# Twelve conditioning slots in one place, and sums that stay in PSUM to the end: a two-block transformer forward on one core

## The reference, cut to what matters

```python
for l in range(2):                                   # block 1
    h = rms_norm(x, norm_mix_pre[l])
    ...                                              # 12 slices of h @ w_in[l]: conformer conv, stick-breaking
    mix = concat([y_conf, y_sb, y_ret, y_sc]) @ w_out[l]   # attention, retention, short conv
    x = x + rms_norm(mix, norm_mix_post[l])
    f = conv_ffn(rms_norm(x, norm_ffn_pre[l]), ffn_up[l], ffn_conv_w[l], ffn_down[l])
    x = x + rms_norm(f, norm_ffn_post[l])
# block 2: c and c_ctx condition it through ada = silu(c) @ ada_w + ada_b, six vectors of 1024
shift1, scale1, g1, shift2, scale2, g2 = split(ada, 6)
u, uc = modulate(rmsnorm(x, norm1_g), shift1, scale1), modulate(rmsnorm(ctx, norm1_g), ...)
x = x + g1 * token_mixer(u, uc, ...)                 # mLSTM both ways, differential attention, branches, w_o
u2 = modulate(rmsnorm(x, norm2_g), shift2, scale2)
x = x + g2 * moe_ffn(u2, ...)                        # 32 experts, the 4 best per token, gated, with biases b2
out = rmsnorm(x, final_g)
```

## Time and profile before

| | |
|---|---|
| median of 3 runs | 2231.74 us (2228.82 to 2232.68) |
| the profiled execution | 2231.71 us, span 2229.9 us |
| mean granted TensorE clock | 0.974 of full speed |
| PE busy | 2046.9 us, 92% of the span |
| DVE, ACT busy | 849.1 us (38%), 610.5 us (27%) |
| DMA | 589.67 MB, mean 264 GB/s |
| GB/s by fortieth of the span | 48 to 328 in the 17th to the 24th, 416 in the 25th, 431 to 433 from the 26th to the 39th |

### The profile page before, as it was taken

The page is one execution under the profiler, slowest core; times in us unless marked ns, Lnnn a source line. Parts: engine busy times, 40 slices in busy tenths (PEclk is TensorE's granted clock), DMA queues, the critical chain, the costliest instruction groups (busy, mean ns, idle before and its releaser), DMA issues.

```text
span 2229.9 us, 27760 instructions
## 1 busy us (share of the span) xinstructions
PE 2046.9 (92%) x11052; PEld 1322.1 (59%) x11052; DVE 849.1 (38%) x1484; ACT 610.5 (27%) x976; POOL 11.6 (1%) x23
## 2 busy tenths in 40 slices
PE   8879999986999799899989999999999999999997
PEld 7838997963999677677779633333333333333332
DVE  5546676663677624744542221111111111111112
ACT  4425555532555523143441110000000000000001
POOL 0000000001000000000000000000000000000000
PEclk9989999998999999899999999999999999999999
DMA  7435553436654325012223679999999999999996
GB/s 286 189 151 181 191 189 134 163 132 219 229 189 164 120 76 198 0 48 95 76 95 151 254 328 416 431 432 431 431 433 431 431 431 432 432 432 432 432 432 258
DMA packets 42081, 589.67 MB, mean 264 GB/s; under 512 B 5120, under 2 KB 5936, under 8 KB 8544
## 3 DMA queue, kind: packets, MB, share of 16 engines
q1 hardware_dynamic: 40304, 583.17, 64.1%
q0 software_dynamic: 1392, 4.93, 0.8%
q10 hardware_dynamic: 288, 0.24, 0.1%
HBM read 587.28 MB, written 1.05 MB: 264 GB/s over the span
## 4 chain that ended last, share of the span: by engine, by line
PE 76%; DMA 12%; DVE 6%; issue 3%; ACT 2%; DVEq 0%; SPq 0%; ACTq 0%
PE psum L1856 45%; PE psum L2247 21%; DMA slots<-exp_w_dram 11%; PE psum L2227 3%; PE psum L2378 3%; PE psum L2284 3%; DVE work L1812 1%; DMA slots<-ffn_up_dram 1%; DVE split_weights L1440 1%; DVE work L1557 0%; DVE split_weights L1260 0%; PE psum L1876 0%; ACT work L889 0%; PE psum L2132 0%; DVE work L1574 0%
## 5 line engine op out<-in xcount | busy, mean ns | idle before, releaser
L2247 PE MATMUL psum<-slots,work 128*64 128x512 f32 x3072 | 676.4, 594 | 60.1 <-DVE work L1812 24.8
L1856 PE MATMUL psum<-split_rows,split_weights 128*128 128x256 f32 (+1 forms) x3744 | 497.4, 295 | 22.9 <-DVE split_weights L1260 11.1
L1856 PEld LDWEIGHTS psum<-split_rows,split_weights 128*128 128x128 f32 x3744 | 478.9, 195 | 46.2 <-DVE split_weights L1260 13.7
L2247 PEld LDWEIGHTS psum<-slots,work 128*64 128x64 f32 x3072 | 219.5, 137 | 481.7 <-issue 480.5
L1260 DVE TENSOR_TENSOR split_weights<-slots,split_weights 128x1024 fp32r<-128x1024 f32 x180 | 218.9, 1223 | 184.0 <-ACT split_weights L922 183.8
L922 ACT ACTIVATE split_weights<-slots 128x1024 fp32r<-128x1024 f32 x180 | 189.6, 1058 | 258.4 <-PE psum L1856 185.6
L1856 PE MATMUL psum<-split_weights,split_rows 128*128 128x512 f32 x1008 | 234.0, 392 | 0.0
L1856 PEld LDWEIGHTS psum<-split_weights,split_rows 128*128 128x128 f32 x1008 | 189.7, 189 | 40.3 <-issue 0.8
L903 ACT ACTIVATE work<-psum 128x512 f32<-128x512 f32 (+3 forms) x182 | 95.6, 536 | 396.2 <-PE psum L2247 254.4
L1817 DVE TENSOR_SCALAR work<-psum 128x512 f32<-128x512 f32 x32 | 22.0, 688 | 424.5 <-PE psum L2247 424.5
L1171 ACT ACTIVATE work<-work 128x512 f32<-128x512 f32 x32 | 20.2, 631 | 499.4 <-DVE work L1817 499.4
(11 more groups left out here) (248 smaller groups left out, 1293.4 us busy)
## 6 DMA issues: line engine op xcount, KB each, us to landing
slots<-exp_w_dram SPq DMA_DIRECT2D x96, 4096.0 KB, 17.5
slots<-w_in_dram SPq DMA_DIRECT2D x56, 1024.0 KB, 4.9
slots<-ffn_up_dram SPq DMA_DIRECT2D x44, 1024.0 KB, 4.8
slots<-ada_w_dram SPq DMA_DIRECT2D x24, 1024.0 KB, 4.9
slots<-ffn_down_dram SPq DMA_DIRECT2D x20, 1024.0 KB, 4.8
slots<-w_out_dram SPq DMA_DIRECT2D x12, 1024.0 KB, 5.0
slots<-w_branch_a_dram SPq DMA_DIRECT2D x4, 1024.0 KB, 7.9
slots<-w_branch_b_dram SPq DMA_DIRECT2D x4, 1024.0 KB, 5.0
```

The costliest lines, as they stand in the source:

```text
L1856: return nc.tensor.matmul(out_, lhsT, rhs, start=first, stop=last)
L2247: return nc.tensor.matmul(b[rows, :], lhs[:, rows], rhs, start=first, stop=last, skip_group_check=True)
```

## The change

- All conditioning slots move into block 2: `LAYER_SLOTS` is 6 in, 2 out and the FFN; `B2_SLOTS` begins with ada 0 to 3, and has 4 and 5 after mq, 6 and 7 before mv 0, 8 and 9 before mv 1, 10 and 11 before mo. All are computed by `ada` and spread or turned by `ada_follow` (mR for rows, mT for columns). The Silu of c moves to the start of `second()`. In block 1 `keep_clock` stands where mod 2, 3 and 4 were.
- In the experts x is added in PSUM: `start_sum` begins each bank YM with identity times x, the biases (multiplied by g2 on DVE beforehand) are added after, and OUT is multiplied by g2 as DVE evacuates it, in place of ACT's copy. ACT's square sums and DVE's final product read the banks, by halves of 512 columns, and SP stores four pieces of 256 KB.
- `fill` of GLU and LIN is done per bank, just before its first product. The last pair is written out by itself; its last 4 MB load is four loads of 1 MB, by rows, and its products go row by row.

```diff
-N_MOD = 5
-LAYER_SLOTS = [("in", s) for s in range(5)] + [("mod", 0), ("in", 5), ("mod", 1), ("out", 0), ("out", 1)]
-LAYER_SLOTS += [("mod", i) for i in (2, 3, 4)]
-OUT_SLOT = LAYER_SLOTS.index(("out", 0))
-FFN_SLOT = len(LAYER_SLOTS)
+LAYER_SLOTS = [("in", s) for s in range(6)] + [("out", s) for s in range(2)]
...
-B2_SLOTS = [("mq", 0), ("mk", 0), ("mv", 0), ("mv", 1), ("ada", 10), ("ada", 11), ("mo", 0), ("mo", 1)]
+
+B2_SLOTS = [("ada", n) for n in range(4)] + [("mq", 0), ("ada", 4), ("ada", 5), ("mk", 0), ("ada", 6), ("ada", 7)]
+B2_SLOTS += [("mv", 0), ("ada", 8), ("ada", 9), ("mv", 1), ("ada", 10), ("ada", 11), ("mo", 0), ("mo", 1)]
...
-            pair(0, 0, True)
-            with eng.Fori(1, PAIRS) as j:
+            pair(0, 0, "first")
+            with eng.Fori(1, PAIRS - 1) as j:
                 pair(j, j)
+            pair(PAIRS - 1, PAIRS - 1, "last")
...
                     src = w["exp_w1_2" if kind == "w1" else "exp_w2_2"][j, q]
                     sp.wait_ge(expert_slot_free, 6 * it + (n + 1))
 
                     sp.sem_inc(expert_load_claimed, 1)
-                    sp.dma_start(expert_place(n), src).then_inc(expert_loaded[n % PAIR_RING], 16)
+                    if part == "last" and n == len(PAIR_SLOTS) - 1:
+                        to, src = (v.rearrange("p (x k n) -> p x k n", x=2, k=4) for v in (expert_place(n), src))
+                        for k in range(4):
+                            sp.dma_start(to[:, :, k, :], src[:, :, k, :]
+                                         ).then_inc(last_rows_loaded[k] if k < 3 else expert_loaded[n % PAIR_RING], 16)
+                    else:
+                        sp.dma_start(expert_place(n), src).then_inc(expert_loaded[n % PAIR_RING], 16)
...
+            for i in range(4):
+                t, half = divmod(i, 2)
+                cut = slice(512 * half, 512 * half + 512)
+                sp.wait_ge(out_ready, i + 1)
+                sp.dma_start(out[t * P:(t + 1) * P, cut], xhat[:, t, cut]).then_inc(out_stored, 16)
+            sp.wait_ge(out_stored, 64)
...
+                ada_rows_out(0, 1, 2, 3)
...
+                ada_rows_out(4, 5)
                 for h in range(NHM):
                     evac(("mk", h), l, m_kT[:, h, :], projected(("mk", h)))
                 evac(("mg", 0), l, gate_parts, take(act, ("mg", 0), l))
+                ada_rows_out(6, 7)
...
-                        if i == 7:
-                            ada_rows_out(10, 11)
-                act.wait_ge(g1_ready, 1)
+                        ada_rows_out(8, 9) if i == 3 else ada_rows_out(10, 11)
...
-                    for n in (0, 1):
-                        evac(("OUT", n), it, out_sb[:, 512 * n:512 * n + 512], take(act, ("OUT", n), it))
-
-                over_pairs(act, pair)
-                rms_of_x(l, 2 * L2 + 3)
+
+                n = over_pairs(act, pair)
+                for half in (0, 1):
+                    for t in range(TT):
+                        act.wait_ge(combined, 3 * PAIRS * n + (1 + t if half else 0))
+                        i = 2 * t + half
...
-                for i in (0, 1, 2):
-                    after_evacuation(dve, ("MT", i), DEPTH - 1)
+                mod_columns(0)
...
+                nc.vector.tensor_tensor(b2_rows[0:N_EXP, :], b2_rows[0:N_EXP, :], g_rows[0:N_EXP, 1, :], ALU.mult
+                                        ).then_inc(b2_scaled, 1)
...
+                    for n in (0, 1):
+                        cut = slice(512 * n, 512 * n + 512)
+                        nc.vector.tensor_tensor(out_sb[:, cut], take(dve, ("OUT", n), it), g_rows[:, 1, cut], ALU.mult
+                                                ).then_inc(evacuated[bank_of(("OUT", n))], 1)
...
+                    for half in (0, 1):
+                        cut = slice(512 * half, 512 * half + 512)
+                        nc.vector.scalar_tensor_tensor(out=xhat[:, t, cut], in0=psum[:, 2 * t + half, :],
+                                                       scalar=rinv[:, t:t + 1], in1=final_row[:, cut],
+                                                       op0=ALU.mult, op1=ALU.mult).then_inc(out_ready, 1)
...
+                ada(0, 1)
+                ada_follow(0)
+                ada(2)
+                ada_follow(1)
+                ada(3)
+                ada_follow(2)
+
+                ada_follow(3)
...
+                def start_sum(i):
+
+                    t, n = divmod(i, 2)
+                    fill(pe, ("YM", i), l)
+                    sum_up(i, ident, x[:, t, 512 * n:512 * n + 512], True)
+
...
                     after_evacuation(pe, ("gT", 0), l)
+                    pe.wait_ge(b2_scaled, 1)
                     for i in range(4):
                         t, n = divmod(i, 2)
-                        fill(pe, ("YM", i), l)
-                        sum_up(i, gT[0:N_EXP, t * P:(t + 1) * P], b2_rows[0:N_EXP, 512 * n:512 * n + 512], True)
...
-                    for key, n, c0 in banks:
-                        fill(pe, (key, n), it)
...
                             key, n, c0 = banks[i]
                             end_of_bank = q == 3 and k == 1
+                            if q + k == 0:
+                                fill(pe, (key, n), it)
...
                     b = fill(pe, ("ST", 0), it)
                     nc.tensor.transpose(b[:, 0:P], pick_gated[:, 0, :], ident).then_inc(expert_slot_free, 1)
                     done(nc.tensor.transpose(b[:, P:T], pick_gated[:, 1, :], ident), ("ST", 0))
...
+                        by_rows = q == 1 and part == "last"
+                        wt = expert_slot(pe, it, 4 + q, 4, not by_rows)
                         if q:
                             after_evacuation(pe, ("AT2", 1), it)
-                        order = [(k, n) for k in range(4) for n in (0, 1)] if q == 0 else [(k, n) for n in (0, 1) for k in range(4)]
+                        order = ([(k, n) for k in range(4) for n in (0, 1)] if q == 0 or by_rows else
+                                 [(k, n) for n in (0, 1) for k in range(4)])
                         for k, n in order:
+                            if by_rows and n == 0:
+                                pe.wait_ge(last_rows_loaded[k], 16) if k < 3 else expert_slot(pe, it, 4 + q, 4)
...
                         for t in range(TT):
                             ins = sum_up(2 * t + n, spread_T[:, t * P:(t + 1) * P], out_sb[:, 512 * n:512 * n + 512])
-                            if (n, t) == (0, 0):
-                                ins.then_inc(expert_slot_free, 1)
-                    ins.then_inc(combined, 1)
+                            ins.then_inc(combined if n + t else expert_slot_free, 1)
...
-                tokens_down("M", l, OUT_SLOT + 1, catT, (4, 5), False, True, None)
-
-                modulation(2)
-                modulation(3)
+                tokens_down("M", l, 7, catT, (4, 5), False, True, None)
+
+                keep_clock(("F", 0), l, 6)
...
+                keep_clock(("F", 0), l, 3)
+                transposed("F", l, 2, idle=(("D", 0), 5))
                 for n in range(MIX_UNITS, len(UNITS)):
```

231 lines of the change are left out of this document (105 added, 126 removed).

## The result

| | before | the change |
|---|---|---|
| median | 2231.74 us (2228.82 to 2232.68, 5 runs) | 2213.7 us (2210.88 to 2219.98, 5 runs) |
| ratio | | 0.9927, 95% interval 0.9908 to 0.9946 |
| profiled execution, span | 2229.9 us | 2216.3 us |
| two more measurements of the change, each beside the kernel before | 2231.57, 2231.86 | 2208.77 (0.9895, 0.9877 to 0.9913), 2207.1 (0.9888, 0.987 to 0.9905) |

The change is faster, by 0.7 to 1.1%. 2204.0 was forecast, -27.7; the three measurements gave -18, -23 and -25. I take its account first, since the prediction was made against such a trace, and the others' beside it.

The account below looks back on a forecast made before the run. Bounds: PE and mixer-end gaps in block 1, PE with short ACT and DVE chains in block 2's token mixer, DMA in the experts. Terms -44.5 + 26.7 + 0.15 - 2.4 - 7.7 = -27.7 gave 2204.0 us, range 2196 to 2216.

Parts of the forecast that it names:

- (a): Block 1, mixer's end to first FFN unit: gap shrinks to 14.6 us, gaining 18.2 and 17.1 in the two layers.
- its sign: Mixer's end: the norm's first square within 1 us of the last tokens_down, first FFN unit 15 us after the mixer.
- (b): Block 1, ACT ahead of the attention's exponentials: removing the Silu and its table load gains 1.5 us per layer.
- (c): Block 1, PE's own work: slot 1 (1.9), turn MT 0 (0.3) and spread MT 2 (0.9) go, 3.1 us per layer.
- (d): Block 2's opening: a chain of turns and slots 2 and 3 delays scale1, +9.4 us, including 1.6 for half clock.
- the first rival: Block 2: opening chain wholly at half clock and one or two slot loads late, +9.5 us, 2213.5; chance 0.15.
- (e): Block 2, slots 4 to 9 with spreads and turns between the projections: cost 17.3 us, ends 12 and 22.
- the sign: Block 2, at mk, mv 0 and mv 1: PE's waits for loads stay under 1 us each.
- The slower rival, the ring: Block 2: added slots delay weight halves, 4.9 us per wait, slower from six waits, 2248 at nine; chance 0.04.
- the term of -2.4: First two expert pairs: bank waits go, -3.3 us, and start_sum(0) adds 0.9, together -2.4.
- (f): Tail after the last load: 22.0 us become 14.3 through loading by rows and finishing by halves, -7.7.
- The rival of four slower loads: Last expert load: four 1 MB loads without overlap land 9.9 us later than one, 2214; chance 0.04.

Follow-up runs that it names:

- before_order: Kernel before, with only ACT's and DVE's splits of a layer's first three FFN units moved behind the second norm's rows; 2203.97 us, 0.9875.
- moe_only: Kernel before with only the change's part from the router on, conditioning slots left in place; 2224.77 us, 0.9974.
- moe_order: before_order with moe_only's part from the router on, all conditioning slots in place; 2199.25 us, 0.9862.
- order2: moe_order with ACT copying slot 3 behind the norm of x, four constant products ahead of slot 3 and the three behind it removed; 2197.51 us, 0.984.
- order2_rows: order2 with both w2 loads of the last pair as four 1 MB loads by rows; 2193.59 us, 0.9828.
- after_clocked: Changed kernel plus products of constants in PE's idle time at block 2's opening, before the attention's product with v and before w_out; 2203.61 us, 0.9872.
- whole_load: Changed kernel with the last 4 MB load in one piece again and its products by banks; 2209.03 us, 0.9901.
- rows_both: Changed kernel with the last pair's fifth load, like its sixth, as four 1 MB loads by rows; 2206.6 us, 0.9895.

## Why the prediction was right, and where its sum was off

**(a), the gap at a mixer's end: right.** 14.6 us were to be left, 15.0 and 15.2 are (14.9 to 15.1 in the others); gains 17.8 and 16.5 of 18.2 and 17.1. The norm's first square was 0.8 us ahead of the mixer's end, as its sign asked (within 1). before_order shows that ACT's order was the cause. It shows too what the prediction didn't ask: the gap needed no slot to move. (The 25.61 us in the earlier trace rows end with the first FFN half; the load at 158.12 that the prediction names is the third unit's, for which ACT waits 1.00 more.)

**(b) and (c), 4.6 us a layer: mis-sized.** From the second layer's transposes to its mixer's end, where 1.5 + 1.9 + 0.3 = 3.7 should have gone, it is 137.4 before and 136.1 in two of three traces of the change, but 133.5 in the third, which is 3.9 less. What took the rest in the two is the clock. Before and after, the attention's product with v and w_out's first 16 products on PE:

```profile
114.60 1.58 PE L1856 MATMUL psum<-work 128*64 128x256 f32 x16 [1.33 <-ACT work L965]
117.05 7.11 PE L1856 MATMUL psum<-slots,work 128*128 128x512 f32 x16 [0.87 <-ACT work L903]
```

```profile
109.55 2.54 PE L1852 MATMUL psum<-work 128*64 128x256 f32 x16 [1.33 <-ACT work L952]
112.88 9.03 PE L1852 MATMUL psum<-slots,work 128*128 128x512 f32 x16 [0.78 <-ACT work L898]
```

1.58 to 2.54 and 7.11 to 9.03: 2.9 us, and 2.9 again in the second layer (2.47 and 9.11); in the third trace the second layer has 1.58 and 7.10. Stretches of the two traces (us; PE, PEld, DVE, ACT, POOL busy; PEclk, DMA share, GB/s), before first:

```profile
110.00:115.00 5.00, 3.67 (x33) 3.44 (x34) 4.64 (x9) 1.49 (x1) 0.00 (x0) 1.00 0.01 2
```

```profile
110.00:115.00 5.00, 4.22 (x17) 2.43 (x14) 5.00 (x13) 0.77 (x2) 0.00 (x0) 0.50 0.00 0
```

The granted clock from 110 to 115 is 1.00 before and 0.50, the 1.2 GHz level, now. Slots 0 and 1 had been PE's work some way ahead of that place. It is no accident of two traces: in the six kernels that keep the slots in block 1 (before, before_order, moe_only, moe_order, order2, order2_rows) all 12 mixers have 1.58 and 7.1; in the seven traces of kernels without them and without constants there, 11 of 14 have 2.5 to 2.9 for the product with v, and 7 of these 8.8 to 9.1 for the products of w_out. after_clocked gives the clock back with constants. The turn MT 0 went as said: PE waits 1.58 us for ACT where it had been. How the 3.7 us divide between the Silu and slot 1 was not tried.

**(d), the opening: 12.8 for 9.4.** The chain began as predicted with the copies behind the norm of ctx, and ran 7.6 us of work in 12.9, from 709.73 to 722.60: 1.6 were put in for the clock, 5.3 were paid. That is the mechanism of the first rival, whose 0.57 stood in the earlier trace rows; that PE would have two slots more to do just before was my argument against it, and 5.02 us of idle stood between. In the third trace the term was 9.7, and 9.7 and 10.2 in whole_load and rows_both: near the forecast. The third trace's chain is 9.7 us long, so it paid 2.1 for the clock.

**(e), the other slots: 18.6 for 17.3**, right: pairs at 3.64, one of four at 5.58 of partly half clock, and one late half at mv 1, where PE waits 1.32 us for the split (the sign had under 1). The slower rival, the ring, did not come: none of these slots waits 4.9 us for a load.

**The experts, -3.6 for -10.** The fills per bank gave 1.9 from the router's start to the first product of w1 (13.1 for 15.0). But the first pair gave it back. Its 16 first products of w2, before and after:

```profile
1326.92 3.65 PE L2247 MATMUL psum<-slots,work 128*64 128x512 f32 x16 [0.69 <-ACT work L903]
```

```profile
1315.96 6.47 PE L2282 MATMUL psum<-slots,work 128*64 128x512 f32 x16 [0.69 <-ACT work L898]
```

2.8 us of half clock and 1.0 for `start_sum(0)`; at the last pair the change is 9.9 us ahead, 10.1 at the router. So the term of -2.4 was +0.1 here. But this half clock is not the change's: before_order, with the experts as they were, has it too (5.35), the twelve other traces have 5.7 to 6.6, and only the trace of before has 3.65. From the router to the last pair's first link in the chain of waits it is 885.4 us before, 886.9 in before_order and 885.5 to 886.0 in the change's three: with the stretch on both sides the term is about -1.

**(f), the tail: -3.7 for -7.7, and this step failed.** "Three of four row blocks are multiplied as they land, leaving 7.09 / 4 = 1.8" forgot what PE does meanwhile. It starts on the fifth load only when that has landed; PE, then DVE:

```profile
2188.24 5.35 PE L2282 MATMUL psum<-slots,work 128*64 128x512 f32 x16 [1.92 <-DMA slots<-exp_w_dram]
...
2194.11 10.52 PE L2282 MATMUL psum<-slots,work 128*64 128x512 f32 x48
2204.66 3.67 PE L2227 MATMUL psum<-work 128*128 128x512 f32 x8
```

```profile
2212.38 1.41 DVE L1837 SCALAR_TENSOR_TENSOR work<-psum,stats,const 128x512 f32<-128x512 f32 x2
```

1.92 us of wait, then without a pause to 2204.6: half of the fifth load's products (5.35, 3.65 at full clock), four transposes, its other half and the sixth's in 10.52. With 9.71 us between two loads and 7.8 us of products for the fifth (both from traces), at most some 1.9 of the sixth's 7.1 can come before its last byte. DMA moves its last bytes in the us from 2197 here, and in that from 2190 in whole_load:

```profile
2197.00:2198.00 1.00, 1.00 (x6) 0.29 (x4) 0.00 (x0) 0.00 (x0) 0.00 (x0) 1.00 0.08 33
```

```profile
2190.00:2191.00 1.00, 1.00 (x6) 0.29 (x4) 0.00 (x0) 0.00 (x0) 0.00 (x0) 1.00 0.24 98
```

So PE has 6.6 to 7.6 us of products left after the last byte where the prediction had 1.8, and whole_load shows the four loads to be worth 0.2 us in the trace. 1.7 us of the term's miss are the half-clock stretch. The rest of the term was right or better: from the end of the sums to the end of the span it is 8.0 us, where the term's pieces add up to 8.9, and 11.3 before. "The last load lands at about 2207.8 either way" holds only measured from the stage before: it landed about 10 us earlier.

The rival of four slower loads had 9.9 us; about 1.5 are there, hidden by PE. In nine traces with the sixth load in four pieces DMA's last bytes came within 9.5 us of PE's start on the fifth load, in whole_load within 8.0.

The forecast's direction and range held; the sum was 14 us off against its own trace: 3.1 in block 1, 3.4 in the opening, 1.3 in the slots, 6.4 from the router on. The prediction had also called itself wrong if the span fell by under 18: the profiled span fell by 13.6, the medians by 18.0, 22.8 and 24.8. The end was to come 14 to 15 us after the last load and came some 18 after. That the first median, 2213.7, is the first rival's 2213.5 is chance: of that rival's 9.5 us the opening gave 3.4 and the slots 1.3, the rest came from places that it does not name.

The largest single cause in that trace is half-clock stretches that the trace of before did not have: 2.9 in each mixer, 5.3 in the opening where 1.6 were counted, 2.8 in the first pair, 1.7 in the last. The mixers' and the opening's came with the change; the first pair's did not, and the last pair's, in 4 of the 12 traces with the change's experts, comes and goes.

## What to carry to other kernels

When a wait ends late because of what stands ahead of it in one engine's program, first try to move the waiting instruction; here that gave 27.6 us at no cost, where moving the ten slots of work cost 28 to 31 us elsewhere. A load cut into pieces helps only if the engine that uses it is idle when they land: subtract its work on the load before. Work that seems free to remove from TensorE may be what keeps its clock up, so price a removal at the granted clock that the stretch behind it may have, and try constants there: here they brought the clock back in the traces, though a gain in time was not shown.

## What the hardware showed that I had not expected

- Gaps as short as 1.33 and 0.78 us in the mixer were followed by a stretch at the 1.2 GHz level that cost 1.2 to 2.9 us, in 11 of 14 mixers of the kernels without slots in block 1. With constants in the gaps, both layers of the one trace were at full clock. The same two gaps (1.33 and 0.87) are in the six kernels with the slots in place, and none of their 12 mixers had such a stretch there. On PE slots 0 and 1 some microseconds ahead are what differs; that these slots are the reason was not tried by itself.
- A switch of ACT's tables shows no drain in the changed kernel either: the load at 696.74 takes 1.28 us and the next activation starts at 698.03, 0.01 behind it. The Trainium skill (ScalarE: Activation LUTs, What ACT_TABLE_LOAD costs) has about 1.4 us of drain a switch; the trace agrees with its 1283 ns for the load alone.
